# Output rows of a residual block: the norm weights multiplied in ahead of the root, two of five pair sums moved to VectorE

## The reference

```python
y = jax.nn.sigmoid(ma) * (o_a @ w_branch_a[l]) + jax.nn.sigmoid(mb) * (o_b @ w_branch_b[l])
y = y @ w_out[l]
x = x + gate[:, None, :] * rms_norm(y, g_post[l])
# rms_norm(v, gain) = v * rsqrt(mean(v * v) + 1e-6) * gain
```

## Time and profile before

| | |
|---|---|
| median of three runs | 904.09 us (901.22, 904.21, 904.09) |
| span of the profiled execution, first to last instruction | 901.7 us (the page gives no time beside it) |
| busy over the span | PE 844.8 us (94%), DVE 597.2 (66%), POOL 495.1 (55%), ACT 472.0 (52%) |
| output stage | 803 to 901.7 us, 28 products |
| mean granted TensorE clock | 0.986 of full speed |

### The profile page before, as it was taken

One profiled execution on the slowest core, in us unless ns is written; L12 is line 12 of the kernel. 1 busy time (PEld: TensorE's weight loads), 2 busy tenths in 40 slices (PEclk: granted clock), 3 DMA queues, 4 the chain that ended last, 5 costly groups with the idle time before them and its releaser, 6 DMA issues.

```text
span 901.7 us, 13090 instructions
## 1 busy us (share of the span) xinstructions
PE 844.8 (94%) x4781; PEld 663.9 (74%) x4781; DVE 597.2 (66%) x700; ACT 472.0 (52%) x861; POOL 495.1 (55%) x373
## 2 busy tenths in 40 slices
PE   2899889999999999999999999999999999989995
PEld 2678667777777777777777777778788888877773
DVE  3888974788694987775887857855310544865554
ACT  7676323786344875436865437755445721325442
POOL 6054655355454545563554544657778521259993
PEclk9999999999999999999999999999999999998998
DMA  9914221102110120120121021111220642120321
GB/s 329 330 49 140 67 74 47 48 1 72 48 47 25 48 61 11 48 71 14 34 71 44 5 71 48 33 38 48 82 82 24 249 148 94 47 91 3 117 93 71
DMA packets 75586, 68.11 MB, mean 76 GB/s; under 512 B 3652, under 2 KB 65156, under 8 KB 75524
## 3 DMA queue, kind: packets, MB, share of 16 engines
q1 hardware_dynamic: 75408, 67.25, 23.2%
q10 hardware_dynamic: 116, 0.03, 0.0%
HBM read 58.88 MB, written 8.39 MB: 75 GB/s over the span
## 4 chain that ended last, share of the span: by engine, by line
PE 72%; DVE 13%; issue 6%; POOL 3%; ACT 2%; SPq 1%; DMA 1%; DVEq 0%; POOLq 0%; ACTq 0%
PE pj L943 15%; PE pj L945 14%; PE pj L944 14%; PE sp L760 4%; PE by L775 3%; PE by L801 2%; DVE acc L1478 2%; DVE k L1621 2%; PE bx L769 2%; POOL w_lo L694 2%; PE sp L980 2%; PE sp L982 2%; PE sp L981 2%; DVE sc L1662 2%; POOL y_all L686 1%
## 5 line engine op out<-in xcount | busy, mean ns | idle before, releaser
L616 POOL TENSOR_TENSOR w_lo<-w_raw,w_hi 128x512 fp32r<-128x512 f32 x140 | 191.8, 1371 | 256.0 <-ACT w_hi L1205 254.4
L943 PE MATMUL pj<-b_hi,w_hi 128*128 128x512 f32 x728 | 307.8, 423 | 15.2 <-issue 4.3
L945 PE MATMUL pj<-b_hi,w_lo 128*128 128x512 f32 x728 | 287.1, 394 | 0.0
L944 PE MATMUL pj<-b_lo,w_hi 128*128 128x512 f32 x728 | 286.5, 394 | 0.0
L943 PEld LDWEIGHTS pj<-b_hi,w_hi 128*128 128x128 f32 x728 | 138.1, 190 | 59.4 <-issue 14.4
L945 PEld LDWEIGHTS pj<-b_hi,w_lo 128*128 128x128 f32 x728 | 138.0, 190 | 31.0
L944 PEld LDWEIGHTS pj<-b_lo,w_hi 128*128 128x128 f32 x728 | 138.7, 190 | 26.5 <-issue 3.1
L1205 ACT ACTIVATE w_hi<-w_raw 128x512 fp32r<-128x512 f32 x132 | 82.8, 627 | 63.5 <-PE pj L945 57.7
L597 POOL TENSOR_TENSOR w_raw<-w_raw,w_raw 128x512 f32<-128x512 f32 x66 | 92.9, 1408 | 4.0 <-DMA w_raw<-in_w_in 1.1
L677 POOL TENSOR_TENSOR wb_lo<-wb_raw,wb_hi 128x512 fp32r<-128x512 f32 x16 | 23.2, 1450 | 62.8 <-ACT wb_hi L1275 62.8
L1220 ACT ACTIVATE p<-sp,cols 128x1024 f32<-128x1024 f32 (+7 forms) x64 | 46.8, 737 | 0.8
(11 more groups left out here) (275 smaller groups left out, 1617.6 us busy)
## 6 DMA issues: line engine op xcount, KB each, us to landing
w_raw<-in_w_in SPq DMA_DIRECT2D x96, 256.0 KB, 4.1
x_in<-in_x SPq DMA_DIRECT2D x8, 512.0 KB, 7.0
ada<-in_w_ada SPq DMA_DIRECT2D x16, 256.0 KB, 7.0
ada<-in_w_ada SPq DMA_DIRECT2D x8, 512.0 KB, 8.2
ada_g<-in_w_ada SPq DMA_DIRECT2D x8, 512.0 KB, 4.0
res<-in_x SPq DMA_DIRECT2D x8, 512.0 KB, 4.3
...
```

The source lines that it names most:

```text
L616: pool.tensor_tensor(w_lo[slot(v)][:, :], raw[:, :], w_hi[slot(v)][:, :].bitcast(F32), ALU.subtract).then_inc(s_wlo, 1)
L943: pe.matmul(bank[:, :], wh, part(b_hi[m], kk), start=(fresh and kk == 0), stop=False, skip_group_check=True)
L944: pe.matmul(bank[:, :], wh, part(b_lo[m], kk), start=False, stop=False, skip_group_check=True)
L945: last = pe.matmul(bank[:, :], wl, part(b_hi[m], kk), start=False, stop=(kk == 3), skip_group_check=True)
```

## The change

1. The row is multiplied by gp_row first (`scale_o`, a tensor_tensor into a new tile `scaled`), while the squares are summed; after the root one instruction computes scaled x root + res (`finish_o`). Before, both instructions stood behind the root.
2. For the last row the early half is squared by ACT and multiplied by gp_row on DVE at x = 5 of the last pair; its part of the mean is prepared. After the last product, its square and its multiplication remain, and one instruction for each half, both on DVE. POOL's addition is gone. The finish of row 6 comes before the steps of the last row, as before.
3. On DVE the finish of row 2t - 1 now stands behind the bank read of M2 (at x = 2); only its multiplication by gp_row stands at x = 1. On ACT the root of row 2t - 1 moves from x = 1 to x = 2.
4. The first and second pair sum of pairs 1 to 3 go from POOL to DVE (`sums_y`, at x = 4 of the pair before). ACT and POOL wait for them on `s_dsum`.

SP's queue is the same but for one semaphore's name, and PE's instructions are the same.

```diff
@@ -715,6 +717,8 @@
                 low_y(v + M2, a12)
                 if t == 0:
                     second_sum_y(0)
+                else:
+                    pool.wait_ge(s_dsum, 2 * t)
                 pool.wait_ge(s_wlo, v + M6)
                 combine_y(a11, s2, a11, ALU.add)
                 low_y(v + M6, s2)
@@ -724,14 +728,6 @@
                 combine_y(a12, a12, a21, ALU.add)
                 low_y(v + M3, a12)
                 low_y(v + M4, a22)
-                if t + 1 < PAIRS_OUT:
-                    first_sum_y(t + 1)
-                    second_sum_y(t + 1)
-
-            pool.wait_ge(s_y2f, NT)
-            pool.wait_ge(s_xr[3], 32)
-            last = rows_o[1][1]
-            pool.tensor_tensor(part(last, 0), part(last, 0), part(res[3], 0), ALU.add).then_inc(s_finp, 1)
 
 
         @block.tensor
@@ -1361,8 +1357,12 @@
                 act.wait_ge(s_proj, ring_at(v))
                 if m in (M1, M2, M4):
                     act.wait_ge(s_ysum, {M1: KT - 1, M2: 2 * KT - 1, M4: 2 * KT}[m])
+                elif t == 0:
+                    act.wait_ge(s_wsum, 5 * (GROUPS - 2) + {M6: 2, M5: 3, M7: 1, M3: 5}[m])
+                elif m in (M6, M7):
+                    act.wait_ge(s_dsum, 2 * t if m == M6 else 2 * t - 1)
                 else:
-                    act.wait_ge(s_wsum, 5 * (g - 2) + {M6: 2, M5: 3, M7: 1, M3: 5}[m])
+                    act.wait_ge(s_wsum, 5 * (GROUPS - 1) + 3 * (t - 1) + (1 if m == M5 else 3))
                 raw = {M1: a11, M2: a12, M6: in_four(y_sum[:, :]), M5: a11, M7: a21, M3: a12, M4: a22}[m]
                 act.activation(in_four(w_hi[slot(v)][:, :]), raw, ACT.Copy).then_inc(s_whj, 1)
@@ -1421,14 +1421,16 @@
                     i = 2 * t - 1
                     act.wait_ge(s_pja, act_reads(n - 1))
                     square_o(i, rows_o[(t - 1) % 2][1][:, :], ss_o[:, i:i + 1])
-                if t and x == 1:
+                if t and x == 2:
                     root_o(2 * t - 1)
+                if t == PAIRS_OUT - 1 and x == PROD - 2:
+                    act.wait_ge(s_pjd, dve_reads(n - 1))
+                    square_o(NT - 2, part(rows_o[1][1], 1), ss_o[:, NT - 1:NT])
                 if x == PROD - 1:
                     i = 2 * t
                     act.wait_ge(s_pjd, dve_reads(n - 1))
-                    square_o(i, rows_o[t % 2][0][:, :], ss_o[:, i:i + 1])
+                    square_o(i if i < NT - 2 else NT - 1, rows_o[t % 2][0][:, :], ss_o[:, i:i + 1])
                     root_o(i)
-            square_o(NT - 1, part(rows_o[1][1], 1), ss_o[:, NT - 1:NT])
             act.wait_ge(s_proj, use(END - 1) + 1)
             square_o(NT, pj[(END - 1) % 2][:, :], t_o)
             root_o(NT - 1)
@@ -1835,32 +1837,38 @@
 
             def norm_o(i):
 
-                t, j = divmod(i, 2)
-                if i == NT - 1:
-                    dve.wait_ge(s_y2s, NT + 1)
-                    then(dve.tensor_tensor(ss_o[:, i:i + 1], ss_o[:, i:i + 1], t_o, ALU.add))
-                else:
-                    dve.wait_ge(s_y2s, i + 1)
+                dve.wait_ge(s_y2s, i + 1 if i < NT - 2 else NT)
                 then(dve.tensor_scalar(ss_o[:, i:i + 1], ss_o[:, i:i + 1], RS / D, EPS * RS, ALU.mult, ALU.add))
                 dve.reciprocal(r_o[:, i:i + 1], ss_o[:, i:i + 1]).then_inc(s_ro, 1)
-                dve.wait_ge(s_rsqo, i + 1)
+
+            def scale_o(i):
+
+                t, j = divmod(i, 2)
                 if i == 0:
                     dve.wait_ge(s_gpr, 1)
+                dve.tensor_tensor(scaled[j][:, :], rows_o[t % 2][j][:, :], gp_row[:, :], ALU.mult).then_inc(s_gps_o, 1)
 
             def finish_o(i):
 
                 t, j = divmod(i, 2)
-                o = rows_o[t % 2][j][:, :]
-                norm_o(i)
-                dve.scalar_tensor_tensor(out=o, in0=o, scalar=r_o[:, i:i + 1], in1=gp_row[:, :],
-                                         op0=ALU.mult, op1=ALU.mult).then_inc(s_y2f, 1)
-                dve.wait_ge(s_y2f, i + 1)
+                dve.wait_ge(s_rsqo, i + 1)
+                dve.wait_ge(s_gps_o, i + 1 if i < NT - 2 else NT)
                 dve.wait_ge(s_xr[i % 4], 16 * (i // 4 + 1))
-                dve.tensor_tensor(o, o, res[i % 4][:, :], ALU.add).then_inc(s_fin, 1)
+                dve.scalar_tensor_tensor(out=rows_o[t % 2][j][:, :], in0=scaled[j][:, :], scalar=r_o[:, i:i + 1],
+                                         in1=res[i % 4][:, :], op0=ALU.mult, op1=ALU.add).then_inc(s_fin, 1)
+
+            def sums_y(t):
+
+                a11, a12, a21, a22 = [y_tile(j, kh, t) for j in range(2) for kh in range(2)]
+                dve.tensor_tensor(a21, a11, a21, ALU.subtract).then_inc(s_dsum, 1)
+                dve.wait_ge(s_dsum, 2 * t - 1)
+                dve.wait_ge(s_wlo, use(STEPS + PROD * (t - 1) + M6) + 1)
+                dve.tensor_tensor(in_four(y_sum[:, :]), a22, a21, ALU.subtract).then_inc(s_dsum, 1)
 
             dve.wait_ge(s_unit["br"], 4 * KT)
             combine_w(M7, wo_22, wo_12, s_t3)
             low_w(M3, wo_22, 1)
+            last = rows_o[1][1]
             for n in range(STEPS + 1, END):
                 t, x = divmod(n - STEPS, PROD)
                 event(n - 1)
@@ -1869,17 +1877,36 @@
                     low_w(M7, b_raw[M7], 2)
                     low_w(M4, b_raw[M4], 2)
                 if t and x == 1:
+                    dve.wait_ge(s_pja, act_reads(STEPS + PROD * (t - 1) + M4))
+                    scale_o(2 * t - 1)
+                if t and x == 2:
+                    norm_o(2 * t - 1)
                     finish_o(2 * t - 1)
+                if x == 4 and t + 1 < PAIRS_OUT:
+                    sums_y(t + 1)
+                if t == PAIRS_OUT - 1 and x == PROD - 2:
+                    dve.wait_ge(s_pjd, dve_reads(n - 1))
+                    dve.tensor_tensor(part(scaled[1], 1), part(last, 1), part(gp_row, 1), ALU.mult).then_inc(s_gps_o, 1)
                 if x == PROD - 1:
-                    finish_o(2 * t)
-            norm_o(NT - 1)
-            last = rows_o[1][1]
-            for n, src in enumerate((pj[(END - 1) % 2][:, :], part(last, 1))):
-                dve.scalar_tensor_tensor(out=part(last, n), in0=src, scalar=r_o[:, NT - 1:NT], in1=part(gp_row, n),
-                                         op0=ALU.mult, op1=ALU.mult).then_inc(s_y2f, 1)
-            dve.wait_ge(s_y2f, NT + 1)
+                    dve.wait_ge(s_pjd, dve_reads(n - 1))
+                    scale_o(2 * t)
+                    if t == PAIRS_OUT - 1:
+                        dve.wait_ge(s_y2s, NT - 1)
+                        then(dve.tensor_scalar(part_o, ss_o[:, NT - 1:NT], RS / D, EPS * RS, ALU.mult, ALU.add))
+                    norm_o(2 * t)
+                    if t < PAIRS_OUT - 1:
+                        finish_o(2 * t)
+            finish_o(NT - 2)
+            dve.wait_ge(s_y2s, NT + 1)
+            then(dve.scalar_tensor_tensor(out=ss_o[:, NT - 1:NT], in0=t_o, scalar=RS / D, in1=part_o, op0=ALU.mult, op1=ALU.add))
+            dve.reciprocal(r_o[:, NT - 1:NT], ss_o[:, NT - 1:NT]).then_inc(s_ro, 1)
+            dve.tensor_tensor(part(scaled[1], 0), pj[(END - 1) % 2][:, :], part(gp_row, 0), ALU.mult).then_inc(s_gps_o, 1)
+            dve.wait_ge(s_rsqo, NT)
+            dve.wait_ge(s_gps_o, NT + 1)
             dve.wait_ge(s_xr[3], 32)
-            dve.tensor_tensor(part(last, 1), part(last, 1), part(res[3], 1), ALU.add).then_inc(s_fin, 1)
+            for half in (1, 0):
+                dve.scalar_tensor_tensor(out=part(last, half), in0=part(scaled[1], half), scalar=r_o[:, NT - 1:NT],
+                                         in1=part(res[3], half), op0=ALU.mult, op1=ALU.add).then_inc(s_fin, 1)
 
 
 _INS = ["x", "c", "w_ada", "b_ada", "g_pre", "g_post", "w_in", "lb_logits", "hg_norm_gain", "lambda_q1", "lambda_k1",
```

More of the change, by code:

```diff
@@ L277, in build @@
         sq_o = block_at("sq_o", 28)
+        scaled = [block_at(f"scaled{j}", (52, 30)[j]) for j in range(2)]
         rows_o = [[block_at(f"rows_o{z}{j}", 36 + 2 * z + j) for j in range(2)] for z in range(2)]
@@ L313, in build @@
         mx, nm, den, rden, c1 = col(2), col(4), col(4), col(2), col(1)
-        ss_o, r_o, t_o = col(NT), col(NT), col(1)
+        ss_o, r_o, t_o, part_o = col(NT), col(NT), col(1), col(1)
         assert used[0] <= 256
@@ L401, in build @@
         s_rsqo = sem("s_rsqo")
-        s_y2f = sem("s_y2f")
         s_xr = [sem(f"s_xr{n}") for n in range(4)]
-        s_fin, s_finp = sem("s_fin"), sem("s_finp")
+        s_fin = sem("s_fin")
+        s_gps_o = sem("s_gps_o")
+        s_dsum = sem("s_dsum")
         s_out = [sem(f"s_out{n}") for n in range(2)]
@@ L1393, in _, with square_o @@
                     y_high(STEPS + M1)
-            def square_o(i, src, dst):
-                if i:
-                    act.wait_ge(s_y2s, i)
+            def square_o(k, src, dst):
+                if k:
+                    act.wait_ge(s_y2s, k)
```

2 lines of the change are left out of this document (1 added, 1 removed).

## The result

The changed kernel takes 893.74 us, the median of four runs (892.72 to 894.19), against 903.85 for four runs of before (901.22 to 904.21). The ratio is 0.9894, with a 95% interval of 0.9872 to 0.9916: faster by 1.1%. The profiled execution took 894.0 us, its span 892.0; so 2.0 us lie around the span, and the 2.4 us by which before's median stands above its span is mostly this offset. The text ahead of the prediction sets before's profiled execution 0.5 us above the fastest run; that holds a span against whole times. With an offset of 1.8 to 2.0, as in all thirteen later profiles, it stands at about 903.6, some 2.4 above the fastest.

What follows compares the result with a forecast made beforehand. POOL's instructions, sharing a port with DVE, were taken to set the pair period of 20.3 us against PE's 19.04. The terms 0.5 - 4.0 - 2.6 = -6.1 took 904.09 to 898.0 us, range 894.3 to 901.8.

Steps and rivals of the forecast that it cites:

- carry the difference over: Last step: before's median lies 2.4 us above its profiled span; keeping that, 904.09 - 6.1 gives 898.0.
- a trio that falls low: Whole kernel: if the middle of three timed runs falls low, the forecast is 895.1 instead of 898.0.
- the third case: Output stage: all stalls go because DVE's sums miss POOL's addition for M3, 1.5 us more won, 896.5; chance 0.12.
- the end, -2.6: Last product's end to span end: 7.1 us instead of 9.73, last DMA issued at E + 4.3; bounds -2.0 and -3.0.
- The start of pair 1: DVE's first sum runs ahead of POOL's addition for M3, so low M3 ends late: +0.5 us.
- Pairs 1 to 3: Output stage after 827.00: stalls fall from 5.13 to 1.1 us, -4.0; bounds -5.1 and -0.6.
- my table: Predicted times of DVE's and POOL's alternating instructions in a pair, counted from T, the end of the previous pair's product M3.
- The price of a sum on DVE: Pair sums moved to DVE: one sum taken as 0.55 us, bounds 0.3 and 1.3; expected to show as 0.55 to 1.2.
- Edits "at nothing": Even rows' earlier multiplication, ACT's early half-row square, the later root and the waits for `s_dsum`: no change in time.
- The port as the bound: Pairs: the port shared by DVE and POOL keeps the period at 20.1 to 20.3 us, total 901.5; chance 0.18.
- the slower case: New waits ahead of M3 in pairs 0 to 2 let the clock fall, 2.9 us each, total 906.7; chance 0.04.
- That nothing is won: Pairs: POOL's freed time goes to waiting for ACT, stalls return on the bank, 902 with the tail's gain; chance 0.06.

Runs made afterwards that it cites:

- the end alone: The kernel before with only rows 6 and 7 finished the new way; ratio 0.9965 to before, stage 95.53 us, E to end 6.50.
- the late sums: The changed kernel with DVE's two pair sums one product later, at x = 5 instead of x = 4; ratio 0.9903 to before, median 894.35 us, stage 90.28.

## Why the prediction was wrong in number, and where it held

**What failed: the last step, "carry the difference over", and the range built on it.** The sum -6.1 was applied to one execution of before as if the 800 us ahead of the output stage would be the same again; their scatter was put at nothing, but for a trio that falls low or not. The runs show in its place: two executions of one kernel lie up to 7.6 us apart (900.15 to 907.71 in twelve runs of before), and the stretch ahead of the output stage took 800.1 to 805.0 us over fourteen profiles. (No profile caught the longest runs, so where their time lies is not shown.) Of the 3.6 us by which the span of 892.0 lies below the 895.6 of my sum, 2.6 are this, and 1.0 is the sum: the stage became 7.0 to 7.1 us shorter, not 6.1. The last 0.7 of the 4.3 us is what was carried over: the 2.4 us between before's span and its median were 1.8 to 2.0 of an offset that every profiled execution has, and in after the median lies 1.7 above the span.

The low end was miscounted too. A low trio takes the forecast from 898.0 to 895.1, 2.9 less; taken off the third case's 896.5 that is 893.6, not 894.3. The measured 893.74 lies just above it, but that would have been luck: the third case did not happen. Run again, the change took 896.28 against 903.37, within the range. That 2.64 us is within the chance of an execution is shown by the second profile of the change (802.98, as late as before's first). What makes the clock come back sooner or later at 100 us stays open.

**The other term that was mis-sized: the end, -2.6, measured -3.26** (9.73 to 6.50 with the end alone). The chain came as worked out: square out of the bank to E + 0.9 with its read of the sum, multiplication out of the bank over the root (E + 1.8), the halves. The two halves took 1.42 together, as at 0.75 and 0.7; the DMA was issued at E + 4.0, not 4.3. The other half of the miss lies behind it: from the last issue to the end of the span there are 2.5 us, where I kept 2.8. The last two DMAs, 256 KB each, are issued at 888.87 and 889.53 now and at 898.52 and 898.90 in before, so the last has 0.28 us more head room behind the other, which is as much as the difference; that this is the cause no run tested. The DMA of row 6 is issued 2.4 us ahead of the last one and was 4.2 ahead in before, so "as much in front as before" was a misreading, of no effect that the profile shows.

**The start of pair 1: +0.5, measured +0.47.** From the start of the third product of pair 0, M6, to that of M3 it is 11.43 us before and 11.90 after. The stall at M3 of pair 0 grew by 0.67, and six matmuls fewer ran at half rate, so the stall has more in it than the change. The cause, a DVE sum ahead of POOL's addition, is confirmed by the late sums, which take the stall to 0.58.

**Pairs 1 to 3: -4.0, measured -4.26** (5.13 to 0.87, from M4 of pair 0 at 824.81 to the last product at 882.80; the table's -4.28 counts from M3). The joint mechanism held: it needs POOL without the sums and the second finish behind the bank read, and each alone gave 0.5 and 1.3. The new latest is low M3 as forecast, 0.37 and 0.28 us instead of 0.5. In detail the turns began the other way: at 845.30 POOL started its low part 0.01 us ahead of DVE's multiplication and ended after 1.30, so it ran 1.1 us ahead of my table up to low M6 (done at 851.07, or T + 6.74 with T = 844.33, against 7.85). At the end it nearly met the table: low M3 done at T + 16.46, forecast 16.62.

**The price of a sum on DVE.** It reads 1.77 and 1.67 in the profile [0.78 by rows 5], outside the 0.55 to 1.2 that I named as a sign. Yet 0.55 was right for what it costs: POOL's addition of 1.75 from 817.97 ends at 819.72, DVE's sum from 818.60 at 820.27, 0.55 later. The duration of an instruction that starts and is held up includes the wait. By the Trainium skill, "SBUF — State Buffer", section "Who interferes with whom", the shared ports are an exclusive lock, and issue order decides who blocks. This case's traces agree, and add the size: behind a holder 0.55 us for 512 elements on DVE, about 1.1 to 1.2 on POOL. So a sum moved from POOL's 1.29 to DVE does leave the port some 0.7 of its time (an estimate, 1.29 less 0.55).

**Edits "at nothing".** Wrong for the even and odd rows' early multiplication: with DVE's sums at x = 4 it costs 0.9 us, for which I had given no bound. With late sums it does cost nothing.

**The rivals.** The port as the bound (901.5) is refuted: the period is 19.41, not 20.1 to 20.3. All stalls going in pairs 1 to 3 (896.5) is what late sums do, and what the change does with its multiplication behind the root, but not what the change does. The clock did not fall in pairs 1 to 3 (1.00 in the window), and the 0.88 us at 822.00 was followed by a matmul of 0.47: the slower case fell in its place. It was right only that a granted clock can move this kernel by microseconds; the profiles part with it at 95 to 130 us, in both kernels. That nothing is won was wrong.
